# Double-buffered hidden activations, bank-wise gather waits, an interleaved last down product and later constant loads in a two-layer mixture-of-experts trunk

## The reference, cut to what matters

```python
def grouped_moe(x, router_w, router_b, w_gate, w_up, w_down):
    ...
    for e in range(N_EXPERTS):
        h = jax.nn.silu(t @ w_gate[e]) * (t @ w_up[e])
        y = y + combine[:, e:e + 1] * (h @ w_down[e])
    return y.reshape(B, S, D)

for i in range(DEPTH):
    ...
    x = layer_norm(ALPHA * x + mix, ln_mix_g[i], ln_mix_b[i])
    ffn = grouped_moe(x, router_w, router_b, moe_w_gate[i], moe_w_up[i], moe_w_down[i])
    x = layer_norm(ALPHA * x + ffn, ln_ffn_g[i], ln_ffn_b[i])
```

## Time and profile before

| | |
|---|---|
| median of 3 runs | 1734.02 us (1733.76 to 1738.78) |
| the profiled execution: its own time | 1737.14 us |
| its span, first to last instruction | 1735.3 us |
| mean granted TensorE clock | 0.96 |
| PE busy | 1585.9 us (91%) |
| DVE busy | 668.1 us (39%) |
| ACT busy | 432.7 us (25%) |
| DMA | 531.18 MB, mean 306 GB/s |
| expert part of layer 0, first to last expert product | 417.5 to 878.4 us |
| expert part of layer 1 | 1222.0 to 1708.5 us |

### The profile page before, as it was taken

The page is one execution under the profiler, slowest core; times in us unless marked ns, Lnnn a source line. Parts: engine busy times, 40 slices in busy tenths (PEclk is TensorE's granted clock), DMA queues, the critical chain, the costliest instruction groups (busy, mean ns, idle before and its releaser), DMA issues.

```text
span 1735.3 us, 19026 instructions
## 1 busy us (share of the span) xinstructions
PE 1585.9 (91%) x7841; PEld 934.2 (54%) x7841; DVE 668.1 (39%) x937; ACT 432.7 (25%) x551; POOL 29.4 (2%) x26
## 2 busy tenths in 40 slices
PE   6999999988989999999869999997999999999993
PEld 5888786875344343343338878785434334334331
DVE  4445335535123231323265474455232222222226
ACT  4334335324110111010135353333111110101112
POOL 1000000000000000000022000000000000000000
PEclk9999999997999999999979999898999999999997
DMA  9554323555999999999966565345799997998993
GB/s 364 205 194 191 122 97 128 212 182 207 420 427 414 428 427 428 428 428 428 428 261 251 189 224 182 131 165 224 282 428 428 427 428 308 422 375 361 429 427 142
DMA packets 47316, 531.18 MB, mean 306 GB/s; under 512 B 5361, under 2 KB 5905, under 8 KB 7938
## 3 DMA queue, kind: packets, MB, share of 16 engines
q1 hardware_dynamic: 45234, 518.08, 73.4%
q0 software_dynamic: 2000, 11.95, 1.9%
HBM read 527.91 MB, written 2.10 MB: 305 GB/s over the span
## 4 chain that ended last, share of the span: by engine, by line
PE 85%; DVE 6%; DMA 3%; ACT 3%; issue 1%; SPq 0%; POOL 0%; DVEq 0%; ACTq 0%
PE bank L1023 37%; PE bank L689 10%; PE bank L690 10%; PE bank L691 10%; PE bank L991 4%; PE bank L1072 4%; DMA w_all<-in_moe_w_down 3%; PE bank L1055 2%; PE bank L823 2%; ACT y_hi L1490 1%; PE bank L1002 1%; DVE X L2094 1%; PE bank L1110 1%; PE bank L896 1%; DMA w_land<-in_ev_w_in 1%
## 5 line engine op out<-in xcount | busy, mean ns | idle before, releaser
L1023 PE MATMUL bank<-w_all,xg 128*64 128x512 f32 x2048 | 454.5, 596 | 1.6 <-DVE hT L2074 1.4
L689 PE MATMUL bank<-w_hi,T_hi 128*128 128x512 f32 x768 | 303.1, 395 | 7.1 <-DVE w_lo L1650 4.6
L690 PE MATMUL bank<-w_lo,T_hi 128*128 128x512 f32 x768 | 301.0, 392 | 0.0
L691 PE MATMUL bank<-w_hi,T_lo 128*128 128x512 f32 x768 | 300.6, 391 | 0.0
L1650 DVE TENSOR_TENSOR w_lo<-w_land,w_hi 128x2048 fp32r<-128x2048 f32 (+1 forms) x96 | 214.2, 2240 | 210.7 <-ACT w_hi L1295 210.6
L1023 PEld LDWEIGHTS bank<-w_all,xg 128*64 128x64 f32 x2048 | 140.9, 137 | 278.3 <-issue 274.3
L1295 ACT CAST w_hi<-w_land 128x2048 fp32r<-128x2048 f32 (+1 forms) x100 | 184.3, 1854 | 247.9 <-PE bank L691 237.0
L1023 PE MATMUL bank<-w_all,hT 128*64 128x512 f32 x992 | 227.6, 602 | 2.2 <-DMA w_all<-in_moe_w_down 2.2
L2094 DVE SCALAR_TENSOR_TENSOR X<-bank,weight,X 128x512 f32<-128x512 f32 x256 | 174.4, 744 | 69.0 <-PE bank L1072 68.9
L2083 DVE TENSOR_TENSOR y_lo<-bank,y_hi 128x512 fp32r<-128x512 f32 x62 | 42.6, 688 | 387.3 <-ACT y_hi L1490 387.3
L689 PEld LDWEIGHTS bank<-w_hi,T_hi 128*128 128x128 f32 x768 | 145.4, 189 | 38.7 <-issue 3.1
(11 more groups left out here) (282 smaller groups left out, 1037.9 us busy)
## 6 DMA issues: line engine op xcount, KB each, us to landing
w_all<-in_moe_w_gate_up SPq DMA_DIRECT2D x128, 2048.0 KB, 15.1
w_all<-in_moe_w_down SPq DMA_DIRECT2D x64, 2048.0 KB, 18.9
w_land<-in_ev_w_in SPq DMA_DIRECT2D x32, 1024.0 KB, 4.8
w_land<-in_od_w_in SPq DMA_DIRECT2D x32, 1024.0 KB, 4.8
w_land<-in_ev_w_out SPq DMA_DIRECT2D x16, 1024.0 KB, 4.8
w_land<-in_od_w_out SPq DMA_DIRECT2D x16, 1024.0 KB, 4.8
w_land<-in_att_w SPq DMA_DIRECT2D x7, 1024.0 KB, 4.7
x0T<-in_xT SPq DMA_DIRECT2D x4, 512.0 KB, 9.7
```

What stands on the lines that cost most here:

```text
L689: pe.matmul(dst, hi_l, hi_r, start=start, stop=False)
L690: pe.matmul(dst, hi_l, lo_r, start=False, stop=False)
L691: return pe.matmul(dst, lo_l, hi_r, start=False, stop=stop)
L1023: ins = pe.matmul(dst[halves[h], :], cols(c), U.weights(q, pos + h)[:, c, :], start=start and c == 0, stop=stop and c == 3)
```

## The change

1. `hT` becomes two buffers, `hT_even` and `hT_odd`. `product(e)` writes the one by the parity of e and waits for the `y_hi` of expert e-2 in place of e-1.
2. The wait ahead of the gather falls. Its first step starts without it; the second step (bank 2) waits for `y_lo` of the first half, the third (bank 3) for that of the second half. The same for `gather_wide`.
3. In the last quad `scatter(2, 1)` goes between the two halves of `down(3)`, and DVE's steps follow that order.
4. SP issues the constants behind the first four full units. POOL issues its six small loads and the first norm rows once 16 units are used. PE and ACT wait for the constants where they first read them.

```diff
-        hT = moe_buf("hT", [P, 4, ALL])
+        hT_even, hT_odd = moe_buf("hT_even", [P, 4, ALL]), moe_buf("hT_odd", [P, 4, CAP])
+        hT = (hT_even, hT_odd)
...
         @block.sync
         def _(sp):
-            sp.dma_start(const[:], A["const"]).then_inc(ident_in, 16)
...
             for j in range(4):
                 load(1, j, unit(w_in0, 0, j))
+            sp.dma_start(const[:], A["const"]).then_inc(ident_in, 16)
...
         @block.gpsimd
+            pool.wait_ge(t_low, 8)
+            pool.wait_ge(used, 16)
             for dst, src in ((rw[:], A["router_w"]),
...
                 pool.dma_start(dst, src, allow_slow_non_contiguous=True).then_inc(const_in, 16)
-            pool.wait_ge(t_low, 8)
             load_rows(A["ln_mix_g"][0:1], A["ln_mix_b"][0:1], 0)
...
         @block.tensor
-            pe.wait_ge(ident_in, 16)
             for j in range(4):
                 pe.wait_ge(t_low, 2 * j + 2)
...
             gemm_block(1, 1)
 
+            pe.wait_ge(ident_in, 16)
             pe.wait_ge(gemm_out_a, 1)
...
-            def gather(Q, n, qs=range(8)):
+            def gather(Q, n, qs=range(8), down_rows=None):
                 for q in qs:
+                    if q in (1, 2) and down_rows is not None:
+                        pe.wait_ge(y_lo_done, down_rows + q - 1)
...
-            def gather_wide(Q):
+            def gather_wide(Q, down_rows):
                 for t in range(KT):
+                    if t in (1, 2):
+                        pe.wait_ge(y_lo_done, down_rows + t - 1)
...
-                    def down(pos, e, following):
+                    def down(pos, e, following, between=None):
...
-                            two_units(pos + 2 * p, bank[2 + p], lambda c: hT[:, c, 0:CAP], True, True)
+                            two_units(pos + 2 * p, bank[2 + p], lambda c: hT[e % 2][:, c, 0:CAP], True, True)
                             if p == 0 and following is not None:
                                 turn(following)
                                 slots(following)
+                            if p == 0 and between:
+                                between()
...
                         pe.wait_ge(slots_out, 4 * Q + 4)
-                        pe.wait_ge(y_lo_done, 2 * (4 * Q + 2) + 2)
                         if is_wide(layer, q, 4):
                             pe.wait_ge(twice_ready, Q + 2)
-                            gather_wide(Q + 1)
+                            gather_wide(Q + 1, 2 * (4 * Q + 2) + 1)
                         else:
-                            gather(Q + 1, 4)
+                            gather(Q + 1, 4, down_rows=2 * (4 * Q + 2) + 1)
                     first_sums(2, 3)
                     if last:
-                        scatter(2, 1)
-                        down(48, 3, None)
+                        down(48, 3, None, lambda: scatter(2, 1))
...
         @block.scalar
-            act.wait_ge(ident_in, 16)
             for j in range(4):
                 act.wait_ge(xT_in[j], 16)
...
+            act.wait_ge(ident_in, 16)
             act.wait_ge(trig_ready, 1)
...
                     def product(e):
                         E = 4 * Q + e
                         dve.wait_ge(silu_done, E + 1)
-                        ge(dve, y_hi_done, 2 * E)
-                        ins = dve.tensor_tensor(hT[:, :, 0:CAP], gsil[:, :, 0:CAP],
+                        ge(dve, y_hi_done, 2 * (E - 1))
+                        ins = dve.tensor_tensor(hT[e % 2][:, :, 0:CAP], gsil[:, :, 0:CAP],
...
                     add(2, 0)
                     if last:
+                        y_out(3, 0)
                         add(2, 1)
-                        down(3, None)
+                        y_out(3, 1)
                         add(3, 0)
```

More of the change, by code:

```diff
@@ L637, in _ @@
         def _(pool):
-            for dst, src in ((rw[:], A["router_w"]),
-                             (rbias[:], A["router_b"].rearrange("(o e) -> o e", o=1).partition_broadcast(P)),
-                             (gains[:, 0, :], A["ev_q_norm"][0].rearrange("(t p) -> p t", t=4)),
-                             (gains[:, 1, :], A["ev_kv_norm"][0].rearrange("(t p) -> p t", t=4)),
-                             (gnorm[:], A["ev_gla_norm"].partition_broadcast(P)),
-                             (posi[:], pos_v)):
-                pool.dma_start(dst, src, allow_slow_non_contiguous=True).then_inc(const_in, 16)
             def load_rows(g, b, n):
@@ L671, in _ @@
             pool.wait_ge(t_low, 8)
+            pool.wait_ge(used, 16)
+            for dst, src in ((rw[:], A["router_w"]),
+                             (rbias[:], A["router_b"].rearrange("(o e) -> o e", o=1).partition_broadcast(P)),
+                             (gains[:, 0, :], A["ev_q_norm"][0].rearrange("(t p) -> p t", t=4)),
+                             (gains[:, 1, :], A["ev_kv_norm"][0].rearrange("(t p) -> p t", t=4)),
+                             (gnorm[:], A["ev_gla_norm"].partition_broadcast(P)),
+                             (posi[:], pos_v)):
+                pool.dma_start(dst, src, allow_slow_non_contiguous=True).then_inc(const_in, 16)
             load_rows(A["ln_mix_g"][0:1], A["ln_mix_b"][0:1], 0)
@@ L1109, in down_wide @@
                                 for c in range(4):
-                                    ins = pe.matmul(bank[2 + h][0:ALL, :], hT[:, c, :], U.weights(q, pos + 2 * p + h)[:, c, :],
+                                    ins = pe.matmul(bank[2 + h][0:ALL, :], hT_even[:, c, :], U.weights(q, pos + 2 * p + h)[:, c, :],
                                                     start=c == 0, stop=c == 3)
@@ L1212, in overflow @@
                         for p in range(2):
-                            two_units(4 + p, bank[2], lambda c: hT[:, c, 0:CAP], True, True)
+                            two_units(4 + p, bank[2], lambda c: hT_even[:, c, 0:CAP], True, True)
                             after(V_, OVER_DVE, ("y", p))
@@ L2072, in product @@
                         dve.wait_ge(silu_done, E + 1)
-                        ge(dve, y_hi_done, 2 * E)
-                        ins = dve.tensor_tensor(hT[:, :, 0:CAP], gsil[:, :, 0:CAP],
+                        ge(dve, y_hi_done, 2 * (E - 1))
+                        ins = dve.tensor_tensor(hT[e % 2][:, :, 0:CAP], gsil[:, :, 0:CAP],
                                                 bank[7][:, 0:4 * CAP].rearrange("p (c s) -> p c s", c=4), ALU.mult)
                         if is_wide(layer, q, e):
-                            ins = dve.tensor_tensor(hT[:, :, CAP:ALL], gsil[:, :, CAP:ALL], bank[6][:, 4 * CAP:8 * CAP]
+                            ins = dve.tensor_tensor(hT_even[:, :, CAP:ALL], gsil[:, :, CAP:ALL], bank[6][:, 4 * CAP:8 * CAP]
                                                     .rearrange("p (c s) -> p c s", c=4)[:, :, MORE:2 * MORE], ALU.mult)
@@ L2168, in overflow @@
                         after(A_, OVER_ACT, "silu")
-                        dve.tensor_tensor(hT[:, :, 0:CAP], gsil[:, :, 0:CAP],
+                        dve.tensor_tensor(hT_even[:, :, 0:CAP], gsil[:, :, 0:CAP],
                                           bank[7][:, 0:4 * CAP].rearrange("p (c s) -> p c s", c=4), ALU.mult) \
```

## The result

| | before | after |
|---|---|---|
| median (lowest to highest), us | 1736.4 (1733.76 to 1740.29), 4 runs | 1711.38 (1710.3 to 1714.17), 4 runs |
| profiled execution, us | 1737.14 | 1711.18 |
| its span, us | 1735.3 | 1709.4 |
| mean granted clock | 0.96 | 0.973 |

The ratio is 0.9866, with an interval of 0.9843 to 0.9888. By it the change takes 1.34% of 1736 us, 23.3 us; the medians differ by 25.0. The forecast was 23 us less and 1711 us.

What follows compares the result with a forecast made beforehand. DMA bounds layer 0 from 737 us; PE bounds layer 1 from about 1434 and nearly everything outside expert parts. Start -5.5, layer 0 -1, layer 1 -16.5: 23 us off 1734.0 gives 1711; range 1701 to a little beyond 1721.5.

Steps and rivals of the forecast that it cites:

- The DMA gains nothing: Layer 0's expert part: PE gains 32 us but the DMA stays full, so its end gains perhaps 0.5 us.
- PE's savings of 32 us plus 5 at the end: Layer 0: 11 product waits of 1.3 us and 3 gathers of 6; up to 5 at the layer's end.
- rival 2: Both layers: PE's waits and low clock all count, with both ends and the start 73 us, to 1661 us; chance 3%.
- 6.6 + 6 - 1.1: Layer 1 behind the wide gather: five product waits 6.6 us, last gather 6, minus 1.1 lost on the last pairs.
- loses some 1.1 us on the last pairs: Late in layer 1: PE comes close to the landings again and loses some 1.1 us.
- the last pair lands as much as 4.9 us later: End of layer 0: norm rows issued earlier share the engines and delay the last weight pair, leaving 0.5 us gain.
- The other bound, 5 us: End of layer 0: the gain if norm rows don't delay the last weight pair, against 0.5 us taken.
- Rival 1: Layer ends: norm rows don't delay the last pair, another 4.5 us in layer 0 and 4 in layer 1; 14%.
- with that 2.4 and 0.8 us to the issue, the unit lands near 12.1: Start: first full unit lands near 12.1 us, its product starts near 16.5, 6.6 us earlier; 5.5 taken.
- Rival 4: Start: ACT and DVE set its pace, so it gives 2 us instead of 5.5, 1714.5 us; chance 7%.
- rival 5: Some twelve experts, both layers: clock falls at nearly every wait for a pair, so slower, up to 1760 us; 3%.
- rival 3: Layer 1: clock falls at two to four new waits, 2.4 us each, some 8 us, 1719 us; chance 16%.

Runs made afterwards that it cites:

- part 2: Only the bank-by-bank gather waits, added to the kernel before: 1731.25 us, ratio 0.9977.
- part 4: Only the later constants, small loads and first norm rows at the start, on the kernel before: 1730.03 us, ratio 0.9978.
- the small loads: Kernel before with only POOL's six small loads, and the first norm rows behind them, issued later: 1732.49 us, ratio 0.9986.
- the constants: Kernel before with only the constants issued behind the first full block: 1733.55 us, ratio 0.9994.
- light loads: Kernels before and after, each loading only the first unit of every down pair: 1730.14 us (0.9975) and 1656.31 us (0.9547).
- late rows: Changed kernel with norm rows issued only once the last weight pair has landed: 1706.64 us (0.9844), on another chip 1705.53 us (0.9838).
- part 3 alone: Only scatter(2, 1) moved between the halves of the last down product, on the kernel before: 1726.84 us, ratio 0.996.
- after light: Changed kernel loading only the first unit of each down pair: 1656.31 us, ratio 0.9547.

## Why the prediction was right, step by step

**The bound of layer 0: right.** "The DMA gains nothing", and 465.2 us came for 466.7. Single executions differ by more: four kernels without the parts 1 and 3 (part 2, part 4, the small loads, the constants) had 468.1 to 468.7 in their layer 0, and the change 465.1 to 466.2. So the gain is 0.5 to 3.7 us. The light loads show it from the other side: PE's savings of 32 us plus 5 at the end, as worked out, were 35.6 there, and 1.5 with full loads. PE met the landings in the second quad, as forecast, with 30.2 us of waits where "20 us or more" was to be seen. They came seven to nine times in a quad of four experts, and not "three or four times an expert". The saving was real and hidden, not absent: that is the difference between the forecast and rival 2, whose 73 us is within some microsecond of the gap of the light kernels (74).

**Layer 1: right, -15.1 for -16.5.** Its terms, by the landmarks: the wide gather with its wait forecast 5, measured 3.78 + 1.6 = 5.4. Ahead of it forecast 0, measured 4.4 - 3.8 = 0.6. Behind it forecast 6.6 + 6 - 1.1 = 11.5, measured 7.8 - 1.6 + 2.9 = 9.1. The step that was too low is "loses some 1.1 us on the last pairs": from 1650 on there are four waits of 6.4 us, one of them 2.59 behind the rows. That is 5.3 us more for a shortfall of 2.4; where PE won the other 2.9 I didn't separate. The two other executions of after had 475.82 and 476.84, 17.4 and 16.4 less than before, so the term was right within what executions differ by. It named the DMA as the bound only up to the wide gather, though; the light loads show that behind it, too, the DMA stood close (half of 33.7 us hidden).

**The ends: right in kind, missized.** The step "the last pair lands as much as 4.9 us later" was too high: it came 2.5 us late. The rows went out at 856.54; the forecast 861 leaves out the start, and 5.5 us earlier at the first gather it is 855.5, so that step held. One pair of the two was on time. Layer 0 as a whole won 1.5 us for a forecast of 1. The other bound, 5 us, is real: the late rows bring layer 0 to 4.1 us below before. Rival 1 was wrong about the change, and describes the version that delays the rows. The wait of 2.61 us, gone when the rows are issued behind the landing, shows that a later request on one queue delayed an earlier one on another. With that the trace agrees with the rule of the Trainium skill (DMA: Bandwidth & Descriptors, "Queues, rings and completion order"), which gives no size for it; that the engines take turns packet by packet no run here shows.

**The start: oversized by one or two.** Forecast 5.5; the unit came 4.6, 3.4 and 3.4 us earlier in the three executions of the change, and the start alone was worth 3.8 us (1.6 to 6.2 by its interval). The step that failed is "with that 2.4 and 0.8 us to the issue, the unit lands near 12.1": ACT used it at 14.18. I had let the 3.8 MB flow at 426 GB/s; the window shows 346. Rival 4's number (2 us) was not far off, but its reason, that ACT and DVE set the pace, isn't what the trace shows: ACT stood idle 1.60 us for the unit.

**The clock: rival 5 fell, and rival 3 came in small.** Over 430 us of layer 0 with its 23 waits for weights the granted clock was 1.00. Of the "two to four such spells" of rival 3 in layer 1 one came, behind the last pair, and cost 5.35 - 3.65 = 1.7 us. The rule beside rival 5, in the Trainium skill (TensorE: Matmul & The Clock Gate, "HAM oscillation — how this bites in real kernels"), tells of a kernel with half clock after every wait for a DMA; its waits were some 3 to 5 us, longer than any in this stream of weights. Behind waits of 0.5 to 1.9 us nothing of the kind is seen here; behind the one of 2.59 us in layer 1 it is, for one half product.

**What the forecast had not got: -3.8 us between the layers.** No part of the change goes with it. Over the 14 executions profiled, the stretch is 333.0 to 333.1 us in five (two of after, and the parts 2, 4 and the constants alone), 336.5 to 336.8 in four (before, part 3 alone, rows late, after light), and between these in the other five, with the same 2.65 us of waiting in each that I compared. Behind that wait the eight instructions took 1.97 us in two executions of the change and 3.39 in the third, so the outcome varies within one kernel; before was profiled once, and there it was 3.75.

**How much of the hit is luck.** Of the 25.9 us between the profiled executions 4.6 are at the unit, 0.9 from there to the first gather, 1.5 in layer 0, 3.8 between the layers and 15.1 in layer 1. The 0.9 and the 3.8 lie in stretches which over the 14 executions ran 385.2 to 391.1 us and 333.0 to 336.8, whatever the kernel. Without them the change has 21.2 us, for a forecast of 23: the start (0.9) and layer 1 (1.4) were too high, layer 0 (0.5) too low. The 23.3 us by the ratio have an interval of 19.4 to 27.3, and two more chips gave 27.2 and 20.5. The mechanism was right; that the sum came within 0.3 us is luck.

## What to carry to other kernels

Where two engines are full at once, count a saving on one of them only in the stretches where the other rests, and look for these stretches in the windows before costing anything; a pair of kernels with lighter loads then tells a hidden saving from one that isn't there. A change that frees an engine earlier also starts whatever that engine releases: here the norm rows, which cost some 2.6 us a layer and more until they were made to wait for the last weight pair; that one wait gives the best version of this study, 1706.3 us over 10 runs. A difference of a few microseconds between two single profiles means little before one knows how far the same kernel differs from itself. Parts of a change don't add: a wait split by banks was worth little while another instruction on DVE was late, and the two together removed both.

## What the runs showed of the hardware

- Waits of PE of 0.5 to 1.9 us, 22 of them in 430 us and most of them 1.2 to 1.3, left the granted clock at 1.00. Behind 2.6 us the outcome varied between executions of one kernel: behind the wait in the mixer eight instructions took 1.97 us or 3.39 (3.75 in before), and behind that for the last pair sixteen took 5.35 us three times and 3.65 three times. The stretch between the layers varied by 3.8 us with it, in kernels that are the same there.
- 2.1 MB of norm rows and the last weight pairs shared the engines, and the last pair was 2.5 us late, about half of the 4.9 us that the rows would take alone at the full rate.
- At the start the DMA share was 0.93 to 0.99 whether it moved 248 or 349 GB/s. A share near 1 didn't tell that the engines moved bytes at their best: the six small loads cost a fifth of the rate beside the constants (257 for 318) and over a quarter without them (248 for 349).
